# Bank rings of a feed-forward and the order of its last chunk, in a two-block layer program on one core

## The reference, cut to what matters

```
def swiglu(h, w_in, w_out):                      # first block, four times, D_FF = 2816
    g, u = jnp.split(h @ w_in, 2, axis=-1)
    return (jax.nn.silu(g) * u) @ w_out

def sqrelu_mlp(h, w1, w2):                       # second block, D_FF_2 = 4096
    return jnp.square(jax.nn.relu(h @ w1)) @ w2
...
x = x + 0.5 * g1 * swiglu(modulate(rms_norm(x, norm_ffn1[l]), sh1, sc1), ffn1_w_in[l], ffn1_w_out[l])
...
x = x + mx[5] * rms_norm_2(sqrelu_mlp(modulate_2(rms_norm_2(x, g[2]), mx[3], mx[4]), mlp_w1[i], mlp_w2[i]), g[3])
if not last:                                     # the context rows, first layer only
    ctx = ctx + mc[5] * rms_norm_2(sqrelu_mlp(...), g[3])
```

## Time and profile before

| | before |
|---|---|
| runs | 2313.72 us median of 3 (2312.96, 2313.72, 2319.47) |
| profiled execution | 2313.62 us, span of its instructions 2311.5 us |
| granted TensorE clock, mean | 0.958 of full speed |
| TensorE matmul (PE) | 2126.4 us busy, 92%, 15149 instructions |
| TensorE weight load (PEld) | 1960.8 us, 85% |
| VectorE (DVE) | 1693.0 us, 73%, 2346 instructions |
| ScalarE (ACT) | 988.0 us, 43%, 1325 instructions |
| DMA | 417.43 MB, mean 181 GB/s |

### The profile page before, as it was taken

How to read it: one execution, slowest core, us unless ns; L and a number is a source line. 1 busy time by engine, 2 the same in 40 slices (tenths; PEclk the granted TensorE clock), 3 DMA queues, 4 the chain that set the end, 5 groups by cost and what they waited for, 6 DMA issues and landing times.

```text
span 2311.5 us, 35613 instructions
## 1 busy us (share of the span) xinstructions
PE 2126.4 (92%) x15149; PEld 1960.8 (85%) x15149; DVE 1693.0 (73%) x2346; ACT 988.0 (43%) x1325; POOL 27.8 (1%) x33
## 2 busy tenths in 40 slices
PE   5899889999999999999998899999999998668998
PEld 4899878999999988799986678877778886558998
DVE  7899777888788868687776665767765667876665
ACT  3433434433543343443354554422222347654443
POOL 0000000000000000000000000000000001100000
PEclk7999999999999999999999999999999999878999
DMA  9899744698698864377663011344564231123661
GB/s 322 279 334 317 221 139 146 223 324 292 220 339 303 287 192 134 122 230 241 226 204 99 1 38 55 125 149 146 170 213 146 66 114 52 46 90 127 212 216 65
DMA packets 338629, 417.43 MB, mean 181 GB/s; under 512 B 9274, under 2 KB 263208, under 8 KB 338472
## 3 DMA queue, kind: packets, MB, share of 16 engines
q1 hardware_dynamic: 335072, 410.79, 53.8%
q10 hardware_dynamic: 3400, 4.38, 0.6%
HBM read 414.09 MB, written 1.05 MB: 180 GB/s over the span
## 4 chain that ended last, share of the span: by engine, by line
PE 43%; DVE 7%; ACT 6%; issue 3%; DVEq 0%; ACTq 0%
PE pb L600 42%; ACT wh L1323 2%; DVE ACC L1928 1%; ACT L_y L1324 1%; DVE RS L2007 1%; PE pb L1168 1%; ACT L1324 1%; DVE wl L1920 1%; DVE T L1928 1%; DVE SM L2505 0%; DVE Hl L1928 0%; DVE L_u L1928 0%; DVE T L1920 0%; ACT A_P L1779 0%; ACT L_x L1324 0%
## 5 line engine op out<-in xcount | busy, mean ns | idle before, releaser
L600 PE MATMUL pb<-Hh,wh 128*128 128x256 f32 (+1 forms) x2624 | 798.5, 304 | 31.6 <-DVE Hl L1928 20.1
L600 PE MATMUL pb<-Hl,wh 128*128 128x256 f32 (+1 forms) x2624 | 783.1, 298 | 0.0
L600 PE MATMUL pb<-Hh,wl 128*128 128x256 f32 (+1 forms) x2624 | 782.6, 298 | 0.0
L1920 DVE TENSOR_TENSOR wl<-raw,wh 128x2048 fp32r<-128x2048 f32 (+3 forms) x271 | 601.1, 2222 | 215.2 <-ACT wh L1323 214.5
L1323 ACT ACTIVATE wh<-raw 128x2048 fp32r<-128x2048 f32 (+3 forms) x271 | 502.3, 1855 | 369.9 <-PE pb L600 294.1
L600 PEld LDWEIGHTS pb<-Hh,wh 128*128 128x128 f32 x2624 | 507.6, 193 | 51.4 <-issue 26.2
L600 PEld LDWEIGHTS pb<-Hl,wh 128*128 128x128 f32 x2624 | 507.9, 194 | 15.0 <-issue 2.2
L600 PEld LDWEIGHTS pb<-Hh,wl 128*128 128x128 f32 x2624 | 507.5, 193 | 12.8
L600 PE MATMUL pb<-Bh,wh 128*128 128x256 f32 (+1 forms) x1376 | 424.8, 309 | 25.0 <-DVE Y L1920 13.5
L600 PE MATMUL pb<-Bl,wh 128*128 128x256 f32 (+1 forms) x1376 | 417.3, 303 | 0.0
L600 PE MATMUL pb<-Bh,wl 128*128 128x256 f32 (+1 forms) x1376 | 416.9, 303 | 0.0
(11 more groups left out here) (245 smaller groups left out, 2011.7 us busy)
## 6 DMA issues: line engine op xcount, KB each, us to landing
raw<-in_ada_w_dram SPq DMA_DIRECT2D x128, 1024.0 KB, 5.7
raw<-in_ffn_w_in_dram SPq DMA_DIRECT2D x88, 1024.0 KB, 6.1
raw<-in_mlp_w_dram SPq DMA_DIRECT2D x64, 1024.0 KB, 5.3
raw<-in_ffn_w_out_dram SPq DMA_DIRECT2D x32, 1024.0 KB, 6.9
raw<-in_mix_w_in_dram SPq DMA_DIRECT2D x22, 1024.0 KB, 5.6
raw<-in_ffn_w_out_dram SPq DMA_DIRECT2D x16, 768.0 KB, 6.0
raw<-in_attn_w_qkv_dram SPq DMA_DIRECT2D x12, 1024.0 KB, 6.1
raw<-in_lru_w_in_dram SPq DMA_DIRECT2D x10, 1024.0 KB, 5.1
```

The lines of the kernel that those rows point to most:

```text
L600: return e.matmul(o, l, r, start=st, stop=sp, skip_group_check=True)
L1920: return e.tensor_tensor(o, a, b, f)
```

## The change

The step order gets a new last chunk: all its inputs, then the output of the chunk before it, then its own output. It holds for all six feed-forwards, since they share `mlp_steps`. In the second block m1 gets two banks and m2 four; the two places that look up an m2 bank by its number follow. The recurrent unit's lr ring keeps its three banks but begins at bank 2.

```diff
--- before.py
+++ after.py
@@ mlp_steps
     for c, n in enumerate(nchunks):
         for j in range(n):
             steps.append(("in", c, j))
-            if j == 0 and c:
+            if j == 0 and 0 < c < len(nchunks) - 1:
                 steps.append(("out", c - 1, 0))
-    return steps + [("out", len(nchunks) - 1, 0)]
+    return steps + [("out", len(nchunks) - 2, 0), ("out", len(nchunks) - 1, 0)]
@@ RING
-        "o2": (0, 1, 2), "m1": (0, 1, 2), "m2": (3, 4, 5), "mf": (0, 1, 2, 3, 4), "my": (5, 3, 4, 0, 1), "lg": (0, 1, 3, 4, 5), "lr": (0, 1, 2), "lw": (3, 4, 5, 6),
+        "o2": (0, 1, 2), "m1": (0, 1), "m2": (2, 3, 4, 5), "mf": (0, 1, 2, 3, 4), "my": (5, 3, 4, 0, 1), "lg": (0, 1, 3, 4, 5), "lr": (2, 0, 1), "lw": (3, 4, 5, 6),
@@ ScalarE, mlp
-                                p = PB[RING["m2"][(n_full - 1) % 3]]
+                                p = PB[RING["m2"][(n_full - 1) % 4]]
```

## The result

The changed kernel takes 2281.13 us, median of 4 runs (2279.11 to 2292.95), against 2316.59 (2312.96 to 2319.94) for the kernel before, measured beside it: ratio 0.9858, 95% interval [0.9818, 0.9897]. It was measured twice more, each time beside the kernel before: 2284.43 (`after_again`, ratio 0.9871 [0.9858, 0.9884]) and 2286.47 (`after_third`, 0.988 [0.9864, 0.9897]). The forecast was 2285.6, a ratio of 0.9879 to the profiled execution. So the change makes the kernel faster by 1.2 to 1.4%, or 27 to 35 us, depending on which of the three measurements is taken.

The account below looks back on a forecast made before the run. TensorE's order of work, busy 92% of the span, was taken as the bound. Gains of 21.3 + 2.5 + 2.6 + 1.6 = 28.0 us against 2313.62 gave 2285.6 us, range 2280 to 2296.5.

Parts of the forecast that it names:

- four output banks: Second block's first feed-forward: four long TensorE stops shrink to under 1 us, two shorter ones vanish; 21.3 us gained.
- last output, second block's first feed-forward: TensorE's 1.74 us wait for the last hidden tile and the low clock after it go; 3.47 us gained.
- new wait on bank 5: Before the second block's first feed-forward's last output, TensorE must wait for VectorE's add on that bank; 0.95 us added.
- three later FFNs: First block: two lose a 0.73 us idle wait, 0.89 us gained each; one has no such wait, 0.
- first FFN: A 1.76 us stop goes, 3.57 us with its clock; two new stops cost 1.9; 1.6 us gained.
- two input banks: Second block's input units: TensorE wants the bank again with 4.6 us in hand, so the cost is 0.
- The anchor: VectorE's add keeps its distance from TensorE's earlier unit, so each long stop shrinks by exactly one fill, 2.72 us.
- Rival B: VectorE has no room; stops move to a weight split or next hidden tile; 17.1 us gained, 2296.5; chance 0.07.
- rival A: Four rests and the new 0.95 us wait each lower the clock, 1.76 us apiece, 8.8 less gained: 2294.4; chance 0.13.
- part 1: Second block's first feed-forward, the four output banks: 21.3 us, including 4 x (2.72 + 1.76) = 17.9 for long stops.
- Rival D: FFNs' new unit order costs what it gives, VectorE lagging some 6 us in the first FFN: 2292.6; chance 0.08.
- Rival C: Two input banks make ScalarE's relu late in input units, 4.4 us a unit, 13 units 57: 2343; chance 0.04.

Follow-up runs that it names:

- rings_only: Kernel before with only the new rings (two input banks, four output banks, lr from bank 2), old step order: 2292.8 us, ratio 0.9903.
- my_first0: Changed kernel with the last output's ring begun on bank 0 (0, 5, 3, 4, 1): 2282.38 us, ratio 0.9866.
- m1_two: Kernel before with two input banks in place of three and nothing else: 2313.75 us, ratio 0.9999.
- m2_two: Kernel before with two output banks in place of three, old order: 2346.82 us, ratio 1.0146.
- adds_first: Changed kernel with VectorE's adds moved ahead of the modulation passes behind the next weight split, second block's first feed-forward: 2291.15 us, ratio 0.9901.
- ffn_old_order: Changed kernel with the first block's four FFNs in their old step order: 2289.35 us, ratio 0.9892.
- adds_unit_a: Changed kernel with the last output's ring begun on bank 0 and VectorE's adds moved earlier only in each output's first unit: 2278.91 us, ratio 0.9849.
- order_only: Kernel before with only the new step order, old rings: 2305.73 us, ratio 0.9958.

## Why the prediction was right, step by step

| step | forecast us | measured us | from |
|---|---|---|---|
| four output banks | 21.3 | 21.2 | `rings_only`, windows |
| last output, second block's first feed-forward | 3.47 | 3.42 | windows |
| new wait on bank 5 | -0.95 | -0.98 | `my_first0` against after |
| three later FFNs | 0.89 + 0.89 + 0 | 1.01 + 0.98 + 0.12 | windows |
| last feed-forward | 0.81 | 0.77 | windows |
| first FFN | 1.6 | 2.05 in this pair; 0.55 or less without the clock | windows |
| two input banks | 0 | 0 | `m1_two` |
| sum | 28.0 | 28.6 | |

- **The anchor.** The step that carried the forecast was that VectorE's lateness hangs on TensorE's earlier unit, so that one bank more takes exactly one fill off the stop. `rings_only` alone gave 21.2 us for it. Forecast rests were 0.66, 0.85, 0.96 and 0.96; measured are 0.58, 0.70, 0.89 and 0.89. The 0.16 that I had added for the overlap was 0.07 to 0.15 too much for what shows as idle. `m2_two` shows the same 2.72 with the other sign. Rival B is refuted for the change: nothing of the stops came back before a weight split or a hidden tile there. How near VectorE is to its limit `adds_first` shows, where another order of its passes brought a stop of 5.29 us.
- **The clock behind the rests** (rival A). It did not fall: granted clock 1.00 from the first to the last output in this run, and likewise in `after_again`, `after_third`, `ffn_old_order`, `rings_only`, `my_first0` and `adds_unit_a`, with 29 spells of 0.55 to 0.89 us together. The section of the Trainium skill that the forecast weighed ("TensorE: Matmul & The Clock Gate", "A second HAM failure mode: psum-queue depth-cycling") reports such falls from another kernel, one in which TensorE idles briefly and often between groups. The forecast had read it as holding for any such rest; for spells up to 0.89 us that come 12 to 139 us apart the trace disagrees, and more frequent ones no run here tried. The margin is not wide. The old stops of 1.74 and 1.76 us had half clock behind them in some executions, so had the 1.28 of `after_third`, and in the first block's mixer so had a stop of 1.17 to 1.18 us that is in all thirteen profiled executions: the granted clock fell behind it in nine, the changed kernel's `after_again` and `after_third` among them, and not in four. The 7 us behind it in the kernel before:

```profile
367.22:374.22 7.00, 6.65 (x53) 4.08 (x54) 6.60 (x26) 6.01 (x28) 0.00 (x0) 1.00 0.00 0
```

and in `rings_only`:

```profile
364.74:371.74 7.00, 7.00 (x36) 3.75 (x36) 5.04 (x19) 5.01 (x23) 0.00 (x0) 0.54 0.00 0
```

- **What was a chance and not a rule.** The forecast priced the fall behind a stop at 1.76 us wherever the one profile showed it. Behind the same stops it came in some executions and not in others (1.73 and 1.76 us in `rings_only`, 2.41 in `m1_two`). For the four long stops this made no difference to the sum: the rests stayed clear in every execution, and in the kernel before the clock had fallen behind all four. Still, the 4 x 1.76 = 7.0 us that part 1 counts for these falls were a likely price and not a sure one. Of the sixteen such stops in `before`, `order_only`, `m1_two` and `m2_two` one, the 3.20 of `order_only`, has no fall behind it, while the 3.41 of `order_only` and one of 3.51 in `m1_two` have a longer one (0.56 and 0.60 of the clock over 7 us). In the first FFN the chance did make a difference.
- **The mis-sized term** is the first FFN's 1.6 us. The mechanism came as forecast: one stop at a weight split and one at a bank of the output, at 0.58 and 0.40 us instead of 1.0 and 0.9. What went, though, was 1.76 of idle time without a sure fall of the clock, so 0.55 at most are the order's own, and this pair reached 2.05, and with it the forecast, only because the fall happened to be in the one profile of before. The forecast had no term for the DMA there, whose late landing made the stop in `after_third`. Rival D is wrong all the same: the order as a whole gains, 8.5 us in `order_only`, though the first FFN's stretch is in three of eight executions longer than the old order's without a fall.
- **Rival C** fell with `m1_two`. In the changed kernel ScalarE's wait for T before its copy to Bh is 67.6 us in 32 waits, the longest 7.2, as in the earlier trace rows, and TensorE has no new idle time before an input unit.

The 35 us of the first measurement is above the forecast because both medians moved apart by a few microseconds; the other two gave 29.8 and 27.5. The two halves add up to 30.0 less the bank wait of 1.0, about 29. What stays open is why the clock falls behind a stop in one execution and not behind the same stop in the next. I did not find a cause in the profiles.

## What to carry to other kernels

When an engine waits for a bank, ask what the late reader itself hangs on. If that is the waiting engine's own earlier work, the stop is a fixed distance less the ring's length in fills; a bank more takes exactly one fill off, a bank less adds one. An order of steps that hides one wait can make a new one where two rings meet in the same bank, so read the bank numbers across the seam. Before an add is moved ahead of filler work, look for whoever waits for the filler: it may be due as well.

## What the runs showed of the hardware that was not expected

- TensorE's stops repeat between executions and kernels within some hundredths of a microsecond (3.41, 3.41 and 3.42 us for one stop in three kernels). The half clock behind them does not: behind 1.17 us the granted clock over 7 us was 1.00 before and 0.54 in `rings_only`, behind 1.76 us it was 0.76 in one run and 1.00 in another, behind 2.41 us 1.00 and 0.76. The 29 spells of 0.55 to 0.89 us in the second block's first feed-forward never had it. One profile prices the idle time well and the clock badly.
- One stretch, a last output and a mixer, took 153.03 us in one execution and 156.04 in another of the same kernel, at 0.97 and 0.95 of the clock. A difference of 3 us in one stage of one profile is therefore no finding by itself.
